# Three edits to the order of work around TensorE in a two-layer hybrid kernel: mixing weights in two parts, four pieces sharing operand chunks, recurrence steps moved

## The reference

```python
mixed = (g_conv * conv_out + g_ssm * ssm_out) @ w_out        # MIX pieces
x = x + rms_norm(mixed, mix_post_g)
h = rms_norm(x, ffn_pre_g)
gt, up = split(h @ w_gate_up); f = (silu(gt) * up) @ w_down  # UP1, DOWN1
x = x + rms_norm(f, ffn_post_g)
# second layer
z = rms_norm(x, norm1_g) @ w_in
lru_x, lru_gate, sc_b, sc_c, sc_x = split(z)                 # LRUX, LRUG, SC
lru_x = causal_dwconv4(lru_x) + b
r = sigmoid(lru_x @ wa + ba); i = sigmoid(lru_x @ wx + bx)   # per head
a = exp(-8 r softplus(-lam))
hid = scan(a, sqrt(1 - a*a) * i * lru_x)                     # recurrence over tokens
y = concat(hid * gelu(lru_gate), sc_b * causal_dwconv3(sc_c * sc_x)) @ w_out
```

## Time and profile before

| what | us |
|---|---|
| median of 3 runs | 976.68 (976.21 to 976.94) |
| the profiled execution, its own time | 977.22 |
| its span in the trace | 975.4 |
| PE busy / PEld busy | 954.8 (98%) / 915.6 (94%) |
| DVE busy / ACT busy | 692.3 (71%) / 512.8 (53%) |
| chain that ended last: PE / issue / DVE / ACT | 61% / 24% / 9% / 4% |

### The profile page before, as it was taken

How to read it: one execution, slowest core, us unless ns; L and a number is a source line. 1 busy time by engine, 2 the same in 40 slices (tenths; PEclk the granted TensorE clock), 3 DMA queues, 4 the chain that set the end, 5 groups by cost and what they waited for, 6 DMA issues and landing times.

```text
span 975.4 us, 19110 instructions
## 1 busy us (share of the span) xinstructions
PE 954.8 (98%) x7139; PEld 915.6 (94%) x7139; DVE 692.3 (71%) x1252; ACT 512.8 (53%) x846; POOL 14.1 (1%) x24
## 2 busy tenths in 40 slices
PE   8999999999999999999999999999999999999997
PEld 6999999999998988899999999999987999999996
DVE  5799999999988633566666545697715888888433
ACT  5537666677755331465665434477303665656320
POOL 0000000000000000000000000000000000000000
PEclk8999999999999999999999999999999999999999
DMA  7476334554452534636555655155235555555501
GB/s 289 157 259 197 130 124 158 194 194 131 170 189 97 189 130 151 217 137 207 173 181 185 216 179 182 50 194 178 84 129 185 204 185 182 177 188 177 212 0 43
DMA packets 45177, 161.50 MB, mean 166 GB/s; under 512 B 5028, under 2 KB 6216, under 8 KB 45000
## 3 DMA queue, kind: packets, MB, share of 16 engines
q1 hardware_dynamic: 43632, 155.02, 46.2%
q10 hardware_dynamic: 1496, 5.80, 1.6%
HBM read 159.72 MB, written 1.09 MB: 165 GB/s over the span
## 4 chain that ended last, share of the span: by engine, by line
PE 61%; issue 24%; DVE 9%; ACT 4%; DMA 1%; POOL 0%; DVEq 0%; ACTq 0%; POOLq 0%
PE A L363 11%; PE A L364 10%; PE A L365 10%; PE A L376 6%; PE B L569 5%; PE B L365 3%; PE B L363 3%; PE B L364 3%; PE B L719 3%; DVE w_lo L1112 2%; PE B L709 1%; DVE part L1148 1%; ACT dec L845 1%; PE A L479 1%; PE A L550 1%
## 5 line engine op out<-in xcount | busy, mean ns | idle before, releaser
L363 PE MATMUL A<-h_lo,w_hi 128*128 128x256 f32 x1472 | 423.8, 288 | 3.5 <-DVE h_lo L1484 1.3
L364 PE MATMUL A<-h_hi,w_hi 128*128 128x256 f32 x1472 | 416.8, 283 | 0.0
L365 PE MATMUL A<-h_hi,w_lo 128*128 128x256 f32 x1472 | 416.8, 283 | 0.0
L1112 DVE TENSOR_TENSOR w_lo<-raw,w_hi 128x1024 fp32r<-128x1024 f32 x242 | 294.1, 1222 | 105.0 <-ACT w_hi L748 104.0
L748 ACT ACTIVATE w_hi<-raw 128x1024 fp32r<-128x1024 f32 x242 | 253.0, 1052 | 107.6 <-PE B L365 54.3
L363 PEld LDWEIGHTS A<-h_lo,w_hi 128*128 128x128 f32 x1472 | 282.3, 192 | 7.7 <-issue 2.8
L364 PEld LDWEIGHTS A<-h_hi,w_hi 128*128 128x128 f32 x1472 | 282.5, 192 | 0.2
L365 PEld LDWEIGHTS A<-h_hi,w_lo 128*128 128x128 f32 x1472 | 282.3, 192 | 0.0
L365 PE MATMUL B<-hid_hi,w_lo 128*128 (+1 forms) x368 | 104.2, 283 | 0.0
L363 PE MATMUL B<-hid_lo,w_hi 128*128 (+1 forms) x368 | 104.1, 283 | 0.0
L364 PE MATMUL B<-hid_hi,w_hi 128*128 (+1 forms) x368 | 103.2, 281 | 0.0
(11 more groups left out here) (213 smaller groups left out, 1027.4 us busy)
## 6 DMA issues: line engine op xcount, KB each, us to landing
raw<-in_weights_dram SPq DMA_DIRECT2D x290, 512.0 KB, 3.7
csrow<-cs_dram ACTq DMA_DIRECT2D x9, 512.0 KB, 4.3
x<-in_x_dram SPq DMA_DIRECT2D x2, 512.0 KB, 4.5
bd<-in_lru_w_dram ACTq DMA_DIRECT2D x1, 1024.0 KB, 5.3
out_dram<-m_wide SPq DMA_DIRECT2D x8, 128.0 KB, 2.0
par<-in_params_dram SPq DMA_DIRECT2D x1, 391.0 KB, 5.7
cst<-in_consts_dram SPq DMA_DIRECT2D x1, 320.0 KB, 6.3
wdt<-in_w_dt_dram SPq DMA_DIRECT2D x1, 128.0 KB, 7.4
```

What stands on the lines that cost most here:

```text
L363: mm(dst, wh, lo, start=first, stop=False, skip_group_check=free)
L364: mm(dst, wh, hi, start=False, stop=False, skip_group_check=free)
L365: return mm(dst, wl, hi, start=False, stop=last, skip_group_check=free)
L1112: V.tensor_tensor(w_lo[:, s, :], raw[:, s, :], w_hi[:, s, :].bitcast(F32), ALU.subtract).then_inc(lo_ready, 1)
```

## The change

MIX pieces leave `NATIVE` and are split; ACT and DVE make `h_hi` and `h_lo` of `mixed` during PW. `scaled_start` becomes `scaled_four`: four pieces share the operand chunks, the fifth follows, then one norm sum (its squares are added up on DVE now) and the spread inside the sixth; the first eight pieces of UP1 and of LRUX have a bank each. Gate products go through two banks (A1, A2) only, after the eight LRUX pieces, and ACT drains them in the SC pieces; the wide steps of the recurrence move from SC to LRUG pieces.

```diff
-NATIVE = frozenset(GLU_NATIVE) | frozenset([LOOP0 + 8 * i + n for i in range(GROUPS - 1) for n in OUT_AT]) | frozenset(range(TAIL0, UP1)) | frozenset(range(OUT2, UP2))
+NATIVE = frozenset(GLU_NATIVE) | frozenset([LOOP0 + 8 * i + n for i in range(GROUPS - 1) for n in OUT_AT]) | frozenset(range(TAIL0, MIX0)) | frozenset(range(OUT2, UP2))
...
+        UP1_BANKS = [A[n][:, 0:T] for n in range(4)] + [B[:, n, 0:T] for n in (1, 2, 0, 3)]
+        LRU_BANKS = [A[n][:, 0:T] for n in range(3)] + [B[:, n, 0:T] for n in range(4)] + [A[3][:, 0:T]]
+        SC_BANKS = [A[0][:, 0:T]] + [B[:, n, 0:T] for n in range(4)] + [A[3][:, 0:T]]
+        GATE_BANKS = [A[n][:, 0:T] for n in (1, 2, 0, 3)]
+
+        def block_bank(c):
+            return A[1 + c % 2]
...
+            def scaled_four(p, operand, summed_n, norm_n, banks, norm_bank):
+                pe.wait_ge(lo_ready, split_order(p + 3))
                 for k in range(KD):
                     pe.wait_ge(operand_ready, operand + k + 1)
-                    for j in range(2):
-                        ins = tile((p + j) % RING, k, h_hi[:, k, :], h_lo[:, k, :], A[j][:, 0:T], k == 0, k == KD - 1)
+                    for j in range(4):
+                        ins = tile((p + j) % RING, k, h_hi[:, k, :], h_lo[:, k, :], banks[j], k == 0, k == KD - 1)
                         if k == KD - 1:
                             ins.then_inc(pieces_done, 1)
-                    if k:
-                        sum_square(n0, k - 1)
-                sum_square(n0, KD - 1)
-                pe.wait_ge(lo_ready, split_order(p + 2))
+                chunk_piece(p + 4, 0, banks[4], h_hi, h_lo)
+                summed_squares(summed_n, norm_bank)
+                pe.wait_ge(lo_ready, split_order(p + 5))
                 for k in range(KD):
                     if k == 5:
-                        spread_scale(norm_n)
-                    ins = tile((p + 2) % RING, k, h_hi[:, k, :], h_lo[:, k, :], A[2][:, 0:T], k == 0, k == KD - 1)
+                        spread_scale(norm_n, norm_bank)
+                    ins = tile((p + 5) % RING, k, h_hi[:, k, :], h_lo[:, k, :], banks[5], k == 0, k == KD - 1)
                 ins.then_inc(pieces_done, 1)
...
                 else:
-                    pe.wait_ge(squares_ready, 2 * KD + m - 2)
-                native_piece(MIX0 + m, ring_bank(72 + m), mixed, mixed_ready if m == 0 else None)
-            spread_residual(3, 11, B[:, 0, :])
+                    pe.wait_ge(m_copied, m - 2)
+                chunk_piece(MIX0 + m, 0, ring_bank(72 + m), h_hi, h_lo, KD if m == 0 else None)
...
-            scaled_start(UP1, KD, 3 * KD, 12)
+            scaled_four(UP1, 2 * KD, 4, 12, UP1_BANKS, B[:, 3, :])
             pe.wait_ge(rs_ready, 1)
-            chunk_piece(UP1 + 3, 0, A[3][:, 0:T], h_hi, h_lo)
-            for j in range(2, 4):
-                up_pair(UP1, j, 0, staged, STAGED_FFN1 + j - 1)
-            with pe.Fori(1, UP1_TURNS) as i:
+            for n in (6, 7):
+                chunk_piece(UP1 + n, 0, UP1_BANKS[n], h_hi, h_lo)
+            for j in range(4):
+                up_pair(UP1, j, 1, staged, STAGED_FFN1 + (1, 2, 5, 6)[j])
+            with pe.Fori(2, UP1_TURNS) as i:
                 for j in range(4):
                     up_pair(UP1, j, i, staged, i * 4 + (STAGED_FFN1 + j - 1))
             for j in range(UP1_TURNS * 4, KF):
...
-                mm(whole_bank(c)[:, 0:T], bd[:, c, 0, :], xp[:, c, 0:T], start=True, stop=True)
-                mm(whole_bank(c)[:, T:2 * T], bd[:, c, 1, :], xp[:, c, 0:T], start=True, stop=True).then_inc(bd_ready, 1)
-
-            scaled_start(LRUX0, ops, 5 * KD, 14)
+                if c >= 2:
+                    pe.wait_ge(bd_drained, c - 1)
+                mm(block_bank(c)[:, 0:T], bd[:, c, 0, :], xp[:, c, 0:T], start=True, stop=True)
+                mm(block_bank(c)[:, T:2 * T], bd[:, c, 1, :], xp[:, c, 0:T], start=True, stop=True).then_inc(bd_ready, 1)
+
+            scaled_four(LRUX0, ops, 6, 14, LRU_BANKS, A[3])
+            chunk_piece(LRUX0 + 6, 0, LRU_BANKS[6], h_hi, h_lo)
             pe.wait_ge(rs_ready, 2)
-            for c in range(3, KD):
-                chunk_piece(LRUX0 + c, 0, eight_banks(c), h_hi, h_lo)
-                if c >= 4:
-                    block_gates(c - 4)
+            chunk_piece(LRUX0 + 7, 0, LRU_BANKS[7], h_hi, h_lo)
+            for c in range(2):
+                pe.wait_ge(copied, c + 2)
+                block_gates(c)
+            consumed = sc_copied, sc_x_used, sc_ready
             for n in range(3 * KSC):
-                if n < 8:
-                    pe.wait_ge(bd_drained, n + 1)
+                if n < 6:
+                    pe.wait_ge(copied, n + 3 if n else 1)
                 else:
-                    pe.wait_ge(sc_ready, (n - 8) // 3 + 1)
-                chunk_piece(SC0 + n, 0, eight_banks(n), h_hi, h_lo)
-                if n < 4:
-                    block_gates(4 + n)
+                    pe.wait_ge(consumed[(n - 6) % 3], (n - 6) // 3 + 1)
+                chunk_piece(SC0 + n, 0, sc_bank(n), h_hi, h_lo)
+                if n < KD - 2:
+                    block_gates(n + 2)
+            pe.wait_ge(bd_drained, KD)
             for c in range(KD):
-                pe.wait_ge(sc_ready, (c + 4) // 3 + 1)
-                chunk_piece(LRUG0 + c, 0, eight_banks(c + 4), h_hi, h_lo)
-            pe.wait_ge(gelu_ready, 4)
+                if c == 2:
+                    pe.wait_ge(sc_copied, KSC - 1)
+                elif c == 3:
+                    pe.wait_ge(sc_ready, KSC)
+                elif c >= 4:
+                    pe.wait_ge(scaled, KF + c - 3)
+                chunk_piece(LRUG0 + c, 0, GATE_BANKS[c % 4], h_hi, h_lo)
...
+            def mixed_high(m):
+                act.wait_ge(mixed_ready, m + 1)
+                F(h_hi[:, m, :], mixed[:, m, :], ACT.Copy).then_inc(stage_hi, 1)
+
             for m in range(KD):
                 split_hi(PW0 + m + LEAD)
+                if m >= 2:
+                    mixed_high(m - 2)
+            mixed_high(KD - 2)
+            mixed_high(KD - 1)
...
             for c in range(KD):
                 split_hi(LRUX0 + c + LEAD)
                 lru_first_tap(c)
-                if c >= 5:
-                    lru_gates(c - 5)
             for n in range(3 * KSC):
+                if n < KD:
+                    lru_gates(n)
                 split_hi(SC0 + n + LEAD)
-                if n < 5:
-                    lru_gates(KD - 5 + n)
-                if 5 <= n < 9:
...
-            for m in range(KD + 1):
+            for m in range(KD + 2):
...
+                if m < KD:
+                    split_lo(PW0 + m + LEAD)
+                if m >= 2:
+                    operand_low(hi_n + m - 2, mixed[:, m - 2, :], h_hi[:, m - 2, :], h_lo[:, m - 2, :])
+            hi_n += KD
...
-            residual_scaled(12, 11, "mix_post_g", "ffn_pre_g", hi_n)
+            residual_scaled(12, 11, "mix_post_g", "ffn_pre_g", hi_n, 0, up1_sums, up1_rstd)
+            sum_squares(sq_wide, 3 * KD)
+            moment_of(13, D, RMS_EPS, up1_sums).then_inc(mean_ready, 1)
...
+                    V.tensor_tensor(sc[:, k, :], sc_sum[:, :], sc_bank(n_), ALU.mult).then_inc(sc_ready, 1)
+                if n_ == 9:
                     dve.wait_ge(bd_drained, KD)
                     own.up(V.tensor_tensor(ig[:, :, :], ig[:, :, :], xp[:, :, 0:T], ALU.mult))
-                if n_ == 10:
-
-                    dve.wait_ge(a_ready, 1)
-                    V.scalar_tensor_tensor(th[:, :, :], rg[:, :, :], 1.0, th[:, :, :], ALU.add,
-                                           ALU.mult).then_inc(m2_ready, 1)
...
+            dve.wait_ge(a_ready, 1)
+            V.scalar_tensor_tensor(th[:, :, :], rg[:, :, :], 1.0, th[:, :, :], ALU.add,
+                                   ALU.mult).then_inc(m2_ready, 1)
...
-                if c == 0:
+                if c == 1:
                     dve.wait_ge(mult_ready, 1)
                     after(own.value())
                     after(own.up(V.tensor_tensor(ig[:, :, :], ig[:, :, :], th[:, :, :], ALU.mult)))
-                n = own.up(V.tensor_tensor_scan(xp[:, c, 0:T], a_t[:, c, :], ig[:, c, :], 0.0, ALU.mult, ALU.add))
+                    own.up(V.tensor_tensor_scan(xp[:, 0, 0:T], a_t[:, 0, :], ig[:, 0, :], 0.0, ALU.mult, ALU.add))
                 if c:
+                    n = own.up(V.tensor_tensor_scan(xp[:, c, 0:T], a_t[:, c, :], ig[:, c, :], 0.0, ALU.mult, ALU.add))
                     after(n - 1)
                     lru_output(c - 1)
```

More of the change, by code:

```diff
@@ L402, in first_two, with spread_residual @@
                             ins.then_inc(pieces_done, 1)
-            def sum_square(n0, k):
-                pe.wait_ge(squares_ready, n0 + k + 1)
-                for t in range(TT):
-                    ins = mm(new_sums[:, t:t + 1], sq_wide[:, k, t * P:(t + 1) * P], ones[:, 0:1], start=False,
-                             stop=k == KD - 1, skip_group_check=True)
-                if k == KD - 1:
```

(25 more changed lines are left out.)

92 lines of the change are left out of this document (44 added, 48 removed).

## The result

The changed kernel takes 986.64 us, the median of 4 runs (984.82 to 987.79); the kernel before took 976.81 beside it (976.21 to 979.11, 4 runs). The ratio is 1.009, with a 95% interval of 1.0075 to 1.0106: about 9.8 us slower. 985.8 was forecast, within 982.4 to 989.6. The profiled execution took 987.29 us, and its span is 985.5.

A forecast was written before the change was run, and what follows sets the result against it. TensorE (PE 98% busy) was taken to bound the kernel. -2.7 + 0.3 + 11.5 = +9.1 us on the profiled 977.22 gives 986.3; the median, 0.54 below, is 985.8 us, range 982.4 to 989.6.

The forecast's parts named there:

- MIX, -2.7: MIX's eight pieces, split, take 2.88 us instead of 3.43, less a wait for the last operand chunks: -2.7 us.
- The wait for the last chunks: In MIX, TensorE waits some 1.6 us in three bits, the longest 1.1, for the last operand chunks.
- UP1, +0.3: UP1: shared start leaves -0.5 us after a 3.2 us wait for the seventh piece; lower clock makes it +0.3.
- Second layer, +11.5: LRUX, SC, LRUG: +9.8 us from TensorE's stop at the gate products, +1.7 for half clock: +11.5 us.
- The standstill: TensorE stands still from 646.5 to 656.4 before chunk 2's gate products, waiting for ACT's sigmoids behind chunk 7's tap.
- the half clock behind the standstill: After TensorE's wait at the gate products, the granted clock falls to half, costing 1.7 us.
- The moved recurrence: Recurrence's wide steps in LRUG cost nothing: four pieces have banks, drains are due 11 us after LRUG starts.
- Rival 1: The clock doesn't fall at any of the waits: +6.6, 983.3 us; chance 0.15.
- rival 2: Lower clock costs more, or LRUG's four banks make TensorE wait for DVE: +11 to +13, around 989 us; chance 0.2.
- Rival 3: TensorE isn't held at the gate products of chunk 2: -2.4 to -0.7, 974.3 to 976.0 us; chance 0.06.
- Rival 4: DVE or ACT reach chunk 7 some us earlier than counted: +2 to +5, 979 to 982 us; chance 0.05.

The follow-up runs named there:

- the early split: Sigmoids begun behind chunk 4, plus both parts of UP1's seventh and eighth weight chunks made before the spread-statistics wait, on the changed kernel: 972.92 us.
- LRUX alone: Changed kernel with only both parts of LRUX's seventh and eighth weight chunks made before the wait for the spread statistics: 983.98 us.
- the filled wait: Changed kernel with 34 products of zeros on TensorE between the first SC piece and the gate products of chunk 2: 983.99 us.
- both early splits: Changed kernel with UP1's and LRUX's seventh and eighth weight chunks split early, and sigmoids of chunk c behind the first tap of chunk c + 2: 975.07 us.

## Why the prediction was right, step by step

**MIX, -2.7.** Right: -2.5 in the trace, -3.2 in the medians of the kernel with this edit alone (its interval spans -4.4 to -2.0). The wait for the last chunks was to be 1.6 us in three bits, the longest 1.1; its longest is 0.92, and eight pieces at 2.88 are 23.04 of the 24.92, which leaves 1.9. The granted clock stayed at 1.00 behind it, as priced. (The terms of the working, -4.4 and 1.6, add up to -2.8.)

**UP1, +0.3.** Right: 0.0. The seventh piece waits 3.13 us for `w_lo`, for the 3.2 of the working; the clock behind it was at its lower level, 1.2 GHz. The experiment with the early split gives the worth of both: 132.50 us of UP1 become 534.23 - 406.29 = 127.94, so 4.6, of which 1.4 are the clock's (1.7 in the working). The gain of four shared pieces was real, and this wait and the clock behind it ate it up. That the clock would fall was priced from one sighting, and this term held in part by luck: the same wait of 3.13 us stands in five traces, and behind it the clock fell in four, while in that of LRUX alone it stayed at 1.00 and UP1 took 131.51 us. There the thirteenth piece waits 0.24 us for VectorE, the wait that the working had at up to 0.9.

**Second layer, +11.5.** Right in mechanism and place; measured +12.1. The standstill was to end 656.4 - 614.12 = 42.3 us behind the first LRUX piece: it ends 42.26 behind it. It was to begin 32.4 behind; it begins at 654.38 - 8.24 = 646.14, so 34.0 behind. That is the half clock behind the seventh piece's wait of 3.54, which the working called free since it only shortens this wait, and so it did: 8.24 instead of 9.9, at no cost. What was mis-sized is the half clock behind the standstill: 2.2 us by the filled wait, for the 1.7 of the working, because I took the 3.4 us stretch seen behind a wait of 1.90, and here it was at least 4.6 long. The moved recurrence cost nothing here, as counted; but the reason given (four banks, drains due 11 us later) holds only as long as TensorE is late. In the changed kernel the third drain ends at 709.41 and the seventh LRUG piece starts at 710.77, so 1.4 us were to spare. With TensorE early the LRUG banks were late, by 1.08 us with the sigmoids from chunk 4 on and by 4.01 with both early splits.

The table load took 1.28 us at 652.10, and the sigmoid stands 0.01 behind its end. So where the Trainium skill, in ScalarE: Activation LUTs, section "What ACT_TABLE_LOAD costs", adds 1.38 for a drain, this row has no room for it; the standstill's end, forecast from the rows to 0.1 us, says the same. The measured median, 986.64, lies nearer to the 987.2 that the page would give than to 985.8; by the trace, what was forecast too low is the clock's 0.5 and the 0.6 ahead of MIX, and not the table load.

**The rivals.** Rival 1 (no clock fall, 983.3) did not come; the filled wait imposed it at the gates, not at the two seventh pieces, and gave 983.99. Of rival 2 the half clock behind the gates came, at 0.5 us more than priced; its banks in LRUG came only in the kernels whose TensorE is earlier. Rival 3, TensorE not held at the gates, is what the sigmoids from chunk 4 on make of the kernel: 977.62, where 974.3 to 976.0 was given for it. The upper end held the half clock behind the seventh piece; its stage took 706.75 - 611.72 = 95.03 us where 94.0 was worked out for it, and the 1.0 is one wait in LRUG, which this rival had not counted (the row at 700.90 in that kernel's timeline). Its condition was sound: sigmoids done by about 648, which is 33.9 us behind the first LRUX piece. In that kernel the second sigmoid ends at 645.1, 33.4 behind it, and the products at 645.56 wait for nothing. Rival 4, VectorE or ScalarE at chunk 7 some us earlier, did not come: the standstill ended within 0.1 us of the forecast.

What stays open: where the 0.6 us ahead of MIX come from, which are smaller than the spread of the runs; why the clock fell behind some idle stretches and not behind others as long; and what the recurrence's place in LRUG costs, for no kernel here moves it back.

## What to carry to other kernels

When instructions of several engines are reordered for the sake of one, read the order of each in-order queue for what now stands in front of the signal that somebody waits for: here a two-instruction drain had moved behind two more chunks of work, and a bank ring of two turned that into a stop of TensorE. Moving it forward by three chunks gave back 9.0 us. Give way to the loads and weight preparations that wait for nothing: whatever can be done ahead of a wait for a statistic or for another engine's product goes ahead of it. Together with the sigmoids' order, such moves turned 9.8 us of loss into 11.0 us of gain. And add up waits on one engine only after asking whether the later one ends at a time set elsewhere: then the earlier one is paid already, and removing it first shows little.
